# Block 0 reordered: x normed and transposed ahead of the norm weights, the first modulation group ahead of the keys' weights and the second behind them, a loop with twelve chunks

## The reference, cut to what matters

```
def rms_norm(x, g):
    y = x * rsqrt(mean(x * x, -1) + EPS)
    return y * g

m = silu([c, c_ctx]) @ ada_w[l] + ada_b[l]      # per layer, 6 modulation vectors of 1024
hm = rms_norm(x, norm1_g) * (1 + scale) + shift         # tokens
hc = rms_norm(ctx, norm1_g) * (1 + scale_c) + shift_c   # context tokens
q, k, v, u, gate = split(hm @ ev_w_in)          # 512, 128, 128, 512, 512 columns
k_ctx, v_ctx = (hc @ ev_w_in)[:, 512:768]
q, k: rms norm per head of 64, then rotary embedding (k_ctx: norm only)
attn = softmax(q @ [k_ctx, k].T / 8) @ [v_ctx, v]       # 8 heads, 2 key heads
g = u * sigmoid(gate)
g = depthwise_conv(g, 31 taps) + conv_b
g = silu(layer_norm(g))
x = x + gate1 * (concat(attn, g) @ ev_w_out)
x = x + gate2 * expert_choice_moe(rms_norm(x) modulated)  # 16 experts, 32 tokens each
```

## Time and profile before

| | us |
|---|---|
| median of 3 runs | 1657.12 |
| lowest to highest | 1656.44 to 1658.31 |
| the profiled execution's own time | 1658.83 |
| its span, first to last instruction | 1657.0 |
| TensorE busy | 1459.3 (88%) |
| VectorE busy | 486.3 (29%) |
| ScalarE busy | 338.6 (20%) |
| bytes read | 558.74 MB, 339 GB/s over the span |

### The profile page before, as it was taken

One profiled execution on the slowest core, in us unless ns is written; L12 is line 12 of the kernel. 1 busy time (PEld: TensorE's weight loads), 2 busy tenths in 40 slices (PEclk: granted clock), 3 DMA queues, 4 the chain that ended last, 5 costly groups with the idle time before them and its releaser, 6 DMA issues. The chain is left out here.

```text
span 1657.0 us, 17609 instructions
## 1 busy us (share of the span) xinstructions
PE 1459.3 (88%) x7700; PEld 815.8 (49%) x7700; DVE 486.3 (29%) x746; ACT 338.6 (20%) x514; POOL 118.8 (7%) x113
## 2 busy tenths in 40 slices
PE   4999879888798899799798878888888999999999
PEld 2754632232242342299533323323225767788897
DVE  1787620100100000256501001001004754345443
ACT  1122500110000000233200000000003745554442
POOL 0000010000000000100100000000003044430000
PEclk8999989999989999999899999999999999999999
DMA  9989989999999999994599999999999844244410
GB/s 375 409 327 417 421 346 426 419 428 425 419 428 425 413 430 426 403 402 180 187 429 421 428 428 421 428 426 423 427 425 348 289 152 153 102 152 176 182 51 26
DMA packets 93298, 563.06 MB, mean 340 GB/s; under 512 B 8048, under 2 KB 9448, under 8 KB 53670
## 3 DMA queue, kind: packets, MB, share of 16 engines
q1 hardware_dynamic: 89504, 551.77, 81.7%
q0 software_dynamic: 2384, 9.42, 1.5%
q10 hardware_dynamic: 1334, 0.75, 0.2%
HBM read 558.74 MB, written 3.17 MB: 339 GB/s over the span
## 5 line engine op out<-in xcount | busy, mean ns | idle before, releaser
L2272 PE MATMUL ps<-ring,scratch 128*32 128x512 f32 x2048 | 436.9, 611 | 54.9 <-DMA ring<-in_moe_w_up 27.1
L2272 PEld LDWEIGHTS ps<-ring,scratch 128*32 128x32 f32 x2048 | 129.0, 112 | 349.7 <-issue 342.6
L2251 PE MATMUL ps<-ring,scratch 128*32 128x512 f32 x1024 | 207.7, 607 | 29.8 <-DMA ring<-in_moe_w_down 29.8
L1983 PE MATMUL ps<-ring_parts,scratch_parts 128*128 128x512 f32 x640 | 180.4, 403 | 5.0 <-DVE xT_parts L1228 1.4
L1983 PE MATMUL ps<-scratch_parts,ring_parts 128*128 128x256 f32 x704 | 146.4, 283 | 0.0
L1983 PEld LDWEIGHTS ps<-ring_parts,scratch_parts 128*128 128x128 f32 x640 | 119.4, 189 | 32.5 <-DVE xT_parts L1228 1.6
L2251 PEld LDWEIGHTS ps<-ring,scratch 128*32 128x32 f32 x1024 | 50.6, 111 | 162.6 <-issue 109.8
L625 ACT ACTIVATE ring_parts<-ring 128x2048 fp32r<-128x2048 f32 x56 | 106.4, 1919 | 93.1 <-PE ps L1983 86.6
L474 DVE TENSOR_TENSOR ring_parts<-ring,ring_parts 128x2048 fp32r<-128x2048 f32 x46 | 105.6, 2296 | 54.9 <-ACT ring_parts L625 53.9
L1983 PEld LDWEIGHTS ps<-scratch_parts,ring_parts 128*128 128x128 f32 x704 | 115.0, 189 | 0.3
L1571 DVE TENSOR_TENSOR scratch<-ps,gate_bc 128x512 f32<-128x512 f32 x16 | 11.1, 691 | 252.2 <-PE ps L2251 252.2
(11 more groups left out here) (397 smaller groups left out, 1542.4 us busy)
## 6 DMA issues: line engine op xcount, KB each, us to landing
ring<-in_moe_w_gate SPq DMA_DIRECT2D x64, 2048.0 KB, 31.2
ring<-in_moe_w_up SPq DMA_DIRECT2D x64, 2048.0 KB, 19.2
ring<-in_moe_w_down SPq DMA_DIRECT2D x64, 2048.0 KB, 30.3
ring<-in_ada_w SPq DMA_DIRECT2D x24, 2048.0 KB, 20.9
ring<-in_mlp_w SPq DMA_DIRECT2D x16, 2048.0 KB, 8.9
ring<-in_sc_w_in SPq DMA_DIRECT2D x6, 2048.0 KB, 21.4
ring<-in_w_in SPq DMA_DIRECT2D x6, 2048.0 KB, 20.2
ring<-in_xattn_wkv SPq DMA_DIRECT2D x4, 2048.0 KB, 35.6
```

Of the source, the lines that this page charges most:

```text
L1983: last = mm(out, lhs[x], rhs[y], start=start and n == 0, stop=stop and n == 2)
L2251: last = mm(ps[32 * j:32 * j + 32, banks[half], :], src[:, k, CAP * j:CAP * (j + 1)], w[:, e, col:col + 512], start=(k == 0), stop=(k == K ...
L2272: last = mm(ps[32 * j:32 * j + 32, banks[half], :], src[:, k, CAP * j:CAP * (j + 1)], w[e][:, 0, col:col + 512], start=(k == 0), stop=(k = ...
```

## The change: what it does

Six things, all in block 0:

1. VectorE norms x ahead of its wait for the norm weights, and TensorE transposes x behind chunk 1 of group 0, ahead of chunk 2 and of the transposes of the norm weights.
2. Group 1 (ada0b) is loaded ahead of ev_kv. TensorE does its four chunks between the context's transposes and the keys' products, VectorE copies its rows behind 14 more taps (`TAPS_CTX`).
3. Group 2 (ada0c) is done ahead of the loop too, behind both keys' products, into bank 7. The columns of group 1 are transposed between them, those of group 2 behind the heads' transposes.
4. The context's keys and values go to bank 0 and not 3, with a wait until q has been read from it.
5. The loop has groups 3, 4 and 5, twelve chunks, spread over the rounds as `LOOP_ADA` says (1, 2, 1, 2, 2, 2, 1, 1), with their columns in rounds 2, 4 and 7; it has 3, 2 and 1 taps in place of 4, 3 and 2.
6. The convolution's weights land in another place (`cwrow`, part of `gate_bc`).

```diff
-STREAM = [... ("ev_q", 1), ("ev_kv", 1), ("ada0b", 4),
+STREAM = [... ("ev_q", 1), ("ada0b", 4), ("ev_kv", 1),
           ("ada0c", 4), ("ada1a", 4), ...
-        cwrow = at(5632, d=512)
+        cwrow = gate_bc[:, 512:1024]
-        TAPS_FIRST, TAPS_Q, TAPS_KV, TAPS_LOOP = 40, 30, 14, (4, 3, 2)
+        LOOP_ADA = {0: [(3, 0)], 1: [(3, 1), (3, 2)], 2: [(3, 3)], 3: [(4, 0), (4, 1)], 4: [(4, 2), (4, 3)],
+                    5: [(5, 0), (5, 1)], 6: [(5, 2)], 7: [(5, 3)]}
+        LOOP_COLUMNS = {2: 3, 4: 4, 7: 5}
+        TAPS_FIRST, TAPS_Q, TAPS_CTX, TAPS_KV, TAPS_LOOP = 40, 30, 14, 14, (3, 2, 1)
# SyncE
             sp.dma_start(ctx_rows, ...)
+            modulations(1)
             columns("ev_kv", evw, 1, width=256, col0=512)
-            for g in range(1, len(ADA)):
+            for g in range(2, len(ADA)):
                 modulations(g)
# ScalarE
-            for w, bank in ((0, 2), (1, 3)):
+            for w, bank in ((0, 2), (1, 0)):
# VectorE
+            normed("x", h, rows)
             dve.wait_ge(sem("params_ps"), 2)
             nc.vector.tensor_copy(flat(gcol[:, :, :]), ...)
...
-            normed("x", h, rows)
             ada_rows(0, 0)
...
             transposed("ctx", cT)
+            taps(TAPS_CTX)
+            ada_rows(1, 3)
             taps(TAPS_KV)
...
-            ada_rows(1, 3)
+            mod_cols(1, 3)
+            ada_rows(2, 7)
             dve.wait_ge(sem("ev_qkT_ps"), 2)
             nc.vector.tensor_copy(kT, pb(2)).then_inc(sem("ev_kT"), 1)
-            mod_cols(1, 3)
+            mod_cols(2, 3)
...
-                if q % 2:
-                    ada_rows(2 + q // 2, 3)
-                    mod_cols(2 + q // 2, 3)
+                if q in LOOP_COLUMNS:
+                    ada_rows(LOOP_COLUMNS[q], 3)
+                    mod_cols(LOOP_COLUMNS[q], 3)
# TensorE
-            for q in range(3):
+            for q in range(2):
                 ada(0, q, 0)
+            transposes("x", rows)
+            ada(0, 2, 0)
             pe.wait_ge(sem("gains_in"), 8 * 16)
...
-            transposes("x", rows)
             ada(0, 3, 0)
...
             transposes("ctx", ctx_rows)
+            for c in range(4):
+                ada(1, c, 3)
             arrived(pe, FIRST["ev_kv"])
             pe.wait_ge(sem("param_cols"), 2)
             kv_rows(2, xT).then_inc(sem("ev_part"), 1)
             normed_columns("ctx")
-            used(kv_rows(3, cT))
+            pe.wait_ge(sem("ev_rows"), 2)
+            used(kv_rows(0, cT))
+            ada_columns(1, 3)
+            for c in range(4):
+                ada(2, c, 7)
             pe.wait_ge(sem("ev_rows"), 10)
-            for c in range(4):
-                ada(1, c, 3)
...
-            ada_columns(1, 3)
+            pe.wait_ge(sem("mod_cols"), 2)
+            ada_columns(2, 3)
...
             for q in range(PAIRS):
-                if q % 2 == 0:
-                    pe.wait_ge(sem("mod_cols"), 2 + q // 2)
-                for c in (0, 1):
-                    ada(2 + q // 2, 2 * (q % 2) + c, 3)
+                for g, c in LOOP_ADA[q]:
+                    if c == 0:
+                        pe.wait_ge(sem("mod_cols"), g)
+                    ada(g, c, 3)
...
-                if q % 2:
-                    ada_columns(2 + q // 2, 3)
+                if q in LOOP_COLUMNS:
+                    ada_columns(LOOP_COLUMNS[q], 3)
```

More of the change, by code:

```diff
@@ L70, in constants @@
     return c, m
-STREAM = [("ada0a", 4), ("ev_u", 1), ("ev_gate", 1), ("ev_q", 1), ("ev_kv", 1), ("ada0b", 4),
+STREAM = [("ada0a", 4), ("ev_u", 1), ("ev_gate", 1), ("ev_q", 1), ("ada0b", 4), ("ev_kv", 1),
           ("ada0c", 4), ("ada1a", 4), ("ada1b", 4), ("ada1c", 4), ("ev_out", 2), ("moe0", 24), ("wk", 1),
```

## The result

| | before | after |
|---|---|---|
| median of the runs (range, number) | 1657.03 us (1656.41 to 1658.31, 8) | 1660.71 us (1656.49 to 1664.69, 8) |
| ratio to before, 95% interval | | 1.0026 (1.0014 to 1.0038) |
| traced execution / its span | 1658.83 / 1657.0 | 1660.85 / 1659.1 |
| first projection starts | 37.19 | 33.62 |
| first scores | 108.67 | 113.45 |

The change makes the kernel slower by 0.14 to 0.38%, 3.7 us between the medians; 1659.8 was forecast. The table is the whole story of the traced execution: 3.6 us ahead at the first projection, 4.8 behind at the loop, 3.6 behind at its end, 2.6 at the first expert chunk, and 2.1 at the end of the span. What it doesn't show is the spread: the eight executions of the changed kernel lie 8.2 us apart, those of before 1.9.

A forecast was written before the change was run, and what follows sets the result against it. TensorE's chain through block 0 to its first expert chunk was taken as the bound. Terms: -2.8 + 7.8 - 2.3 + 1.7 - 1.7 = +2.7 us, giving a forecast of 1659.8 us, range 1653.5 to 1664.5.

The forecast's parts named there:

- What bounds the kernel: TensorE's chain through block 0 up to its first use of an expert chunk sets the end, not the transfers.
- the closed hole: Pause in block 0's transfers around 95 us, about 8.5 us; the change closes it, claimed worth nothing in itself.
- rival b: Closing the transfers' pause at 95 us counts: chunks arrive 8.5 us earlier and alone set the end, 1648.6; chance 0.06.
- the second hole: Pause in transfers around 225 us, about 6.4 us, ring full before TensorE's first expert chunk; forecast from near 211 to about 228.
- The start: Start of block 0: with x ahead of the norm weights the first projection starts 2.8 us earlier, bounds 1.3 to 5.
- Rival (d): The start gives nothing, held by TensorE's clock or the load of chunk 3: +5.5 us, 1662.6; chance 0.12.
- The two groups ahead of the loop: Two groups of four modulation chunks before the loop, formerly one: first scores 7.8 us later, bounds 7.4 to 8.5.
- The loop: Twelve chunks instead of sixteen: of 8.5 us less TensorE work about 2.3 us show, bounds 0 to 8.5.
- Rival (a): The loop is TensorE's and gives back all 8.5 us: -5.2 us, 1651.9; chance 0.09.
- The clock: Loop's end: idle time ahead of the last columns halves TensorE's clock, 1.7 us lost, bounds 0 to 3.4.
- rival (c): The clock halves a round earlier, in round 6, costing 4 us more: +6.7 us, 1663.8; chance 0.15.
- The gate: Routing: the second gate's load lands before VectorE needs it, 1.7 us won, bounds 0 to 1.8.

The follow-up runs named there:

- e10: e8 with the second gate's load issued between the two tiles of GpSimd's norm, not behind both: 1649.06 us, ratio 0.9955.
- e7: The changed kernel with group 2 back in the loop (sixteen chunks), only group 1 ahead of the keys: 1662.74 us, ratio 1.0039.
- e2: The changed kernel with SyncE held ahead of the fourth group until six rows of q, keys and values are read: 1662.07 us, ratio 1.0035.
- e6: The changed kernel without its first edit (x normed behind the norm weights, transposed ahead of chunk 3): 1661.63 us, ratio 1.0033.
- e1: The kernel before with only the first edit, x normed and transposed ahead of the norm weights: 1655.68 us, ratio 0.9994.
- e12: The kernel before with the second gate's load issued between the two halves of the norm: 1655.70 us, ratio 0.9991.
- e3: The changed kernel with the same twelve chunks placed 1, 1, 2, 2, 2, 0, 2, 2 over the loop's rounds: 1655.56 us, ratio 0.9996.
- e4: The changed kernel with zero-weight products added, 8 behind round 6's chunk and 16 ahead of round 7's: 1656.00 us, ratio 0.9997.
- e5: e3 with 8 zero-weight products ahead of round 7's last chunk: 1652.25 us, ratio 0.9976.
- e9: The kernel before with 8 zero-weight products ahead of round 7's last modulation chunk: 1655.57 us, ratio 0.9995.
- e8: e5 with the load of ctx issued one place earlier, ahead of ev_q: 1651.73 us, ratio 0.9970.

## Why the prediction held, and which term was off

- **What bounds the kernel.** Shown. From the first use of an expert chunk to the end of the span the traces have 1431.1 us before, 1430.6 after, and 1428.4 to 1430.2 in the experiments, while the first use itself moved between 219.67 (e10) and 233.5 (e7) in them. That is constant to 2.7 us, so the traces can't carry a term smaller than that to the end of the span. The chain of TensorE through block 0 is what the time follows, and the closed hole (rival b) is worth nothing: the changed kernel has it closed and is slower, and reopened in part by e2 it moved no mark of TensorE up to the last columns of the loop. The forecast had the ring some 8 us ahead and the second hole from 211 on; the ring was 3.9 ahead and the hole began at 215.7, since the last chunks waited for slots. That cost nothing, for the same reason.
- **The start, -2.8.** 3.57 us at the first projection, 0.8 more than summed, and 4.5 at the context's transposes (77.31, 81.84 in e6), where the clock's part is in: it is at half for 3.4 us of the first projection and not for 5.2. Of these 2.84 reach the first scores (e6). That this is the 2.8 of the sum is in part luck: on the kernel before the same edit gives 1.3 there (e1). The step's remark that VectorE gets only part of it, beside TensorE's projections, missed that in that kernel VectorE is then the later of the two. The price also varies between executions: in e12, which has the old start, the first projection comes at 35.83 and not 37.19. Rival (d) is refuted by these marks, since the latest of the traces with the new start has it at 34.41 (e7); the medians (0.9 us in e6) can't tell.
- **The two groups ahead of the loop, +7.8.** With the start +5.0 by the sum, 4.78 in the trace. That TensorE and VectorE arrive level at the heads' transposes was right: the wait there is 0.16 us. The split is another than the count suggests: the first group has the whole price, by way of VectorE's head norms, the second none (e7).
- **The loop, -2.3.** 63.93 us against 65.14; 1.64 of the 63.93 are the half clock between the second sums and the next scores, so the layout gave 2.85. From scores to scores rounds 0 to 5 took 5.28, 7.54, 7.13, 7.54, 7.23 and 9.46 us, where 5.4, 7.5, 7.2, 7.5, 7.2 and 9.5 (9.13 of before and 0.4) were summed. Rival (a), 8.5 us, is refuted in this layout; but e3, with the same twelve chunks, took 58.0 us. It was the layout that kept back the gain, not the number of chunks.
- **The clock, +1.7: the term that was mis-sized.** Behind the last columns the trace has 1.6. But the clock also fell in round 6, rival (c)'s place, though only for 3.4 us (1.6 us lost and not 4), so the trace has 3.2 in all. Over the executions the two idle stretches cost 4.7 us, 2.2 to 7.2 by the intervals (e4). The spread of 8 us goes with them in e4 and e5 (3.1 and 2.7); that it is theirs is not shown, since e2 has them and its 5 executions lie 2.0 apart, and e9 has its one filled and its 11 lie 4.3 apart. The term took one fall, from one execution; what it should have held is the mean over falls that come now here, now there, and last 3.4 us in this trace and 10 in e2's. Its premise, that the old loop keeps the clock up, was one execution too: e1 and e12 have the old loop and the fall.
- **The gate, -1.7.** 1.8 in the two traces. Taken from the kernel before by e12 the wait is worth 0.8, so this term may be too good by about 1; the interval of e12 doesn't exclude that it is right.
- **Together.** +2.7 was summed and +2.0 measured between the traced executions (2.1 between their spans); between the medians +3.7. By e4 the changed kernel without the idle clock of rounds 6 and 7 would stand at 1656.00, not told from before; its ratio is 0.9997, that of before with its own last round filled 0.9995 (e9). With the idle time filled in both, the two orders are level within some 2 us: what was moved ahead of the loop and what the start, the loop and the gate give back cancel out, and the loss is the clock. So the direction was right, and the reason was there at half of its size or less.

Term by term the two traces give, forecast in brackets: ahead of the loop +4.8 (+5.0), the loop's layout -2.85 (-2.3), the clock +3.2 (+1.7), the gate -1.8 (-1.7). Two things more were not in the sum. In the routing the clock was at half from 206.2 to 223.4 before and from 211.6 to 225.3 after, 17.2 and 13.7 us; from the gather to the first expert chunk the traces have 8.81 and 8.07 us, -0.7. And from there to the end of the span they have -0.5. That makes +2.1. That the forecast came within 1 us of the median is therefore in part luck: the clock's term was 1.5 us too small in the traces and 3 over the executions, and what made up for it in the traces, 0.5 from the layout and 1.2 from the two unsummed parts, has nothing to do with it.

What stays open: why the clock falls in some executions behind the same idle time and not in others; how often it falls in the kernel before; and how often the gate's wait occurs before.

## What to carry to other kernels

When work is moved out of a loop, the rounds that end in a wait for another engine must keep theirs: there the removed work turns into idle time of TensorE, which then pays again in half clock. Follow the engine that ends last, and not only TensorE: a gain at the start arrives at the loop only as far as VectorE's own chain, here from the landing of ctx, lets it. And a closed hole in the transfers is worth nothing while the ring is full at the next stage's begin; look for the moment from which they run without a break.

## What the runs showed of the hardware

- The same kernel's executions can lie 8.2 us apart (0.5%) with no edit between them. With the idle stretches of the loop filled they lay 3.1 (e4) and 2.7 us (e5) apart. Its two slowest executions (1664.56 and 1664.69) have the lowest mean clock of the eight, 0.960, but 1662.74 has 0.965, as high as any, so the clock is not shown to be all of it. One trace of such a kernel is one draw.
- Idle time of 2.63 us ahead of the last columns was followed by a half clock of 3.4 us in e3, of 6.7 in e1 and of 10.1 in e7 and e12; before, 2.25 us was followed by none. 4.35 us was followed by 3.4 us of it in the changed kernel and by 10.1 in e2 and e6. The 2.80 us ahead of the second sums were followed by a fall in the changed kernel and by none in e6, where the sums took 1.99 us.
- The half clock could last while TensorE was busy without a gap: 10.10 of the 10.10 us from 178.0 on in e2.
- 24 more products of TensorE made a kernel 4.7 us faster.
- The same load of the gate took 5.9 us to land where the ring's last chunk landed 1.0 us ahead of it, 8.1 us in e1, where it landed 0.5 us ahead, and 10.1 to 10.7 us in before, e8, e9, e10 and e12, where that chunk landed behind it.
